# Layer attention of the last two latent blocks behind the first query, and 40 PEER steps more in the second tail

## What is computed

```python
def block(args):                      # window attention, one block of 128 queries
    qi, ki, vi, mi = args
    s_loc = where(mi, einsum(qi, ki) * scale, -inf)      # its own block and both neighbours
    s_ctx = einsum(qi, k_ctx) * scale                    # and all 256 context tokens
    p = softmax_with_sink(concatenate([s_loc, s_ctx]), sink_l)
    return einsum(p[..., :n_loc], vi) + einsum(p[..., n_loc:], v_ctx)

def merge(ys, gates_pre, w_branch, w_out):               # four branches, attention is ys[3]
    acc = sum(sigmoid(gates[i]) * (ys[i] @ w_branch[i]) for i in range(4))
    return acc @ w_out

def block(xb):                        # PEER, one block of 128 tokens
    s = einsum(xb @ wq, keys32)                          # 8 heads, 2 x 128 keys
    expert, cv = top 16 of the 16 x 16 sums of the two top-16 lists
    act = gelu(einsum('nd,nhkd->nhk', xb, u[expert]))    # 128 rows of u for every token
    return einsum('nhk,nhkd->nd', softmax(cv) * act, v[expert])
```

## Time and profile before

| | |
|---|---|
| runs, median (lowest to highest) | 6053.19 us (6052.09 to 6063.03) |
| profiled execution, span | 6280.9 us |
| TensorE, VectorE, ScalarE, GpSimd busy | 4128.8, 3226.1, 711.8, 2794.8 us |
| DMA | 1739.24 MB, 277 GB/s over the span |
| gathers of u and v | 2560, of 512 KB each |

### The profile page before, as it was taken

How to read it: one execution, slowest core, us unless ns; L and a number is a source line. 1 busy time by engine, 2 the same in 40 slices (tenths; PEclk the granted TensorE clock), 3 DMA queues, 4 the chain that set the end, 5 groups by cost and what they waited for, 6 DMA issues and landing times.

```text
span 6280.9 us, 65214 instructions
## 1 busy us (share of the span) xinstructions
PE 4128.8 (66%) x23760; PEld 2525.3 (40%) x23760; DVE 3226.1 (51%) x7726; ACT 711.8 (11%) x1572; POOL 2794.8 (44%) x2606
## 2 busy tenths in 40 slices
PE   5899767777988864544443668888977533333346
PEld 4677544335666652221110235557766300000012
DVE  3422788565625856556444216443277564654430
ACT  1221112123010011000000001233100000000000
POOL 0000243555322446767767630000034677777765
PEclk8999887889998986665555789999988755555557
DMA  6645565988886999999999971112579999999998
GB/s 221 219 156 166 190 208 199 316 312 291 290 302 231 323 340 343 355 352 360 361 367 361 368 262 43 57 43 80 171 257 326 348 353 361 369 358 365 359 367 328
DMA packets 721231, 1739.24 MB, mean 277 GB/s; under 512 B 88912, under 2 KB 371408, under 8 KB 719248
## 3 DMA queue, kind: packets, MB, share of 16 engines
q0 software_dynamic: 380032, 1384.49, 59.9%
q1 hardware_dynamic: 314896, 304.03, 15.4%
q10 hardware_dynamic: 25984, 46.56, 2.1%
HBM read 1706.98 MB, written 27.89 MB: 276 GB/s over the span
## 4 chain that ended last, share of the span: by engine, by line
PE 31%; issue 21%; DMA 10%; POOL 10%; DVE 9%; another core or an unknown queue 2%; ACT 2%; SPq 0%; POOLq 0%; ACTq 0%; DVEq 0%
POOL arena L3090 10%; PE bank L1219 7%; PE bank L1312 6%; DMA arena<-in_peer_v,arena 5%; PE bank L794 4%; PE bank L1273 3%; PE bank L1225 3%; DMA arena<-in_peer_u,arena 3%; DVE arena L2252 2%; PE bank L805 1%; PE bank L876 1%; PE bank L1174 1%; DMA arena<-in_w_in 1%; PE bank L1253 1%
## 5 line engine op out<-in xcount | busy, mean ns | idle before, releaser
L3090 POOL DMA_INDIRECT arena<-in_peer_u,arena x1280 | 1413.4, 1104 | 2173.6 <-DVE arena L2162 951.5
L1312 PE MATMUL bank<-arena 128*32 128x256 f32 x10240 | 1216.4, 541 | 1451.7 <-DMA arena<-in_peer_v,arena 1175.5
L2252 DVE CUSTOM_DVE_ANT_0 arena<-arena 128x1024 f32<-128x1024 f32 x1280 | 1540.5, 1223 | 1013.7 <-DMA arena<-in_peer_u,arena 922.4
L3090 POOL DMA_INDIRECT arena<-in_peer_v,arena x1280 | 1354.6, 1058 | 880.6 <-PE bank L1312 357.6
L1312 PEld LDWEIGHTS bank<-arena 128*32 128x32 f32 x10240 | 311.2, 130 | 2306.7 <-DMA arena<-in_peer_v,arena 1705.3
L1219 PE MATMUL bank<-arena 128*128 128x256 f32 x2560 | 618.3, 397 | 90.7 <-issue 55.8
L794 PE MATMUL bank<-arena 128*128 128x512 f32 (+1 forms) x1600 | 636.9, 552 | 30.2 <-issue 26.6
L1219 PEld LDWEIGHTS bank<-arena 128*128 128x128 f32 x2560 | 504.8, 200 | 187.1 <-issue 108.7
L794 PEld LDWEIGHTS bank<-arena 128*128 128x128 f32 x1600 | 320.4, 207 | 299.5 <-issue 279.4
L1225 PE MATMUL bank<-arena 128*128 128x256 f32 x1280 | 306.5, 382 | 2.3 <-ACT arena L2810 2.3
L1273 PE MATMUL bank<-arena 128*128 128x256 f32 x1280 | 292.6, 390 | 23.2 <-issue 23.2
(11 more groups left out here) (271 smaller groups left out, 3905.3 us busy)
## 6 DMA issues: line engine op xcount, KB each, us to landing
arena<-in_w_in SPq DMA_DIRECT2D x152, 1024.0 KB
arena<-in_mod_w POOLq DMA_DIRECT2D x20, 2048.0 KB, 11.6
arena<-in_peer_wq SPq DMA_DIRECT2D x40, 1024.0 KB
arena<-in_w_branch SPq DMA_DIRECT2D x60, 512.0 KB
arena<-in_w_out SPq DMA_DIRECT2D x20, 1024.0 KB
arena<-in_peer_u,arena POOLq DMA_INDIRECT x1280
arena<-in_peer_v,arena POOLq DMA_INDIRECT x1280
arena<-in_w_branch SPq DMA_DIRECT2D x40, 256.0 KB
```

What stands on the lines that cost most here:

```text
L1312: i = mm(banks[6 + g // 2][32 * j:32 * j + 32, (g % 2) * W:(g % 2 + 1) * W], G["ws"][:, g, 32 * m:32 * m + 32], G["row"][ROW_BUFFER["v", i ...
L2252: v.tensor_tensor_reduce(u, u, G["h2"][it % 2], 1.0, 0.0, ALU.mult, ALU.add, G["dots"][:, n:n + 1]).then_inc(*pr.step("dot", it, n))
L3090: fl.done(eng.indirect_dma_start(G["row"][x], None, table, bass.IndirectOffsetOnAxis(ids[:, n:n + 1], 0)), f"row_landed{x}", (kind + "_lan ...
```

## The change

`attn_mix` takes a half. Before the first tail it now treats blocks 2 and 3 alone (10 units instead of 18). Blocks 4 and 5 are treated at the start of the second tail, 10 units, woven with three of the four branches of that half's merge; the fourth branch follows. There attention takes PSUM banks 0, 1, 2, 6 and 7 and the woven merge banks 3 and 4.

The second tails take ROUTE + 128 + 40 steps of their PEER call, c1 and the part behind t1 40 fewer. For the first 44 slots of the call's second block four u and four v buffers are used. GpSimd's wait for the end of the second query is moved from that block's slot 0 to its slot 44. The routing of the third block is moved from slots 3 to 80 of the second block to slots 43 to 96.

In layer 0 the place of attention's keys and values is used by others in between, so ScalarE's queue stores both (384 KB each) to HBM ahead of the first half and loads them back at the start of the second tail, behind peer0's last store of x. In both layers attention's scores lie over WSP and its keys, values and diagonal over YP and XS; WSP is cleared at slot 116 of a call's first block instead of ahead of the call. The weights of the second half's merge are loaded with the fourth branch last.

```diff
@@ constants and tables @@
+BESIDE = {"attn": (0, 1, 2, 6, 7), "merge": (3, 4)}
...
+AHEAD = 40
+SWITCH = AHEAD + 4
+
+
+def ahead_of(call, it):
+
+    return 0 if call is PC0 or it != call.first + 1 else AHEAD
+
+
+def route_table(start):
+
+    if start == 0:
+        heads = {(16 * (j // 2) + 8 * (j % 2) + k): (what, j) for j in range(HEADS) for k, what in ((3, "keys"), (7, "pairs"))}
+        return {**heads, 64: ("centre",), 68: ("pick", 0), 76: ("pick", 1), 80: ("experts",), 119: ("gates",)}
+    heads = {start + 3 + 5 * j + k: (what, j) for j in range(HEADS) for k, what in ((0, "keys"), (3, "pairs"))}
+    return {**heads, start + 44: ("centre",), start + 46: ("pick", 0), start + 52: ("pick", 1), start + 56: ("experts",),
+            119: ("gates",)}
...
-                for kind, ring, i, step in (("u", u_ring, it, "dot"), ("v", v_ring, it - 1, "v_summed")):
+                few = ahead_of(call, it) and n < SWITCH
+                for kind, ring, i, step in (("u", u_ring[:4] if few else u_ring, it, "dot"),
+                                            ("v", v_ring[:4] if few else v_ring, it - 1, "v_summed")):
...
-                attn_mix=4 * nb + 2, merge=48)
+                attn_mix=4 * len(halves_of(p)[0]) + 2, merge=48)
...
-    if woven(p) and f == 0:
-        return [x for x in every if x[1] < 3], [x for x in every if x[1] == 3]
     if late(p) and f == 0:
         return [x for x in every if x[1]], [x for x in every if x[1] == 0]
-    return [every]
+    return [x for x in every if x[1] < 3], [x for x in every if x[1] == 3]
...
+        ATTN_LOW = SLOTS * 32 + NSCORE + W
...
-            k, v_, s_, pt, dg = lay_low(0, *sizes) if woven(p) else lay(base, *sizes)
+            if woven(p) or f:
+                (s_, pt), (k, v_, dg) = lay_low(0, *sizes[2:4]), lay_low(ATTN_LOW, *sizes[0:2], sizes[4])
+            else:
+                k, v_, s_, pt, dg = lay(base, *sizes)
@@ TensorE @@
-            def attn_mix(p):
+            def attn_mix(p, half):
...
-                seq = [(t, f) for t in blocks_of(p) for f in range(AH // AKV)]
+                seq = [(blocks_of(p)[x], f) for x in halves_of(p)[half] for f in range(AH // AKV)]
+                kept, ring = late(p) and half, "attn" if half else None
+                if kept:
+                    eng.wait_ge(*at("y_scaled", PC0.first + len(PC0.blocks) - 1))
...
-                if p.t0:
+                if kept:
+                    eng.wait_ge(*at("attn_back", p.l))
+                elif p.t0:
                     eng.wait_ge(*at("attn_in", p.l))
...
-                pn, half = p.name, slice(f * W, (f + 1) * W)
+                pn, half, ring = p.name, slice(f * W, (f + 1) * W), "merge" if f and part[0][1] == 0 else None
...
+                        if it == call.first:
+                            for x in (6, 7):
+                                eng.wait_ge(*at("read", last_in[x]))
@@ TensorE, VectorE and ScalarE alike @@
-                yield from weave(attn_mix(p), merge_part(p, 0, merge_parts(p, 0)[0]), u["merge"] / u["attn_mix"])
+                yield from weave(attn_mix(p, 0), merge_part(p, 0, merge_parts(p, 0)[0]), u["merge"] / u["attn_mix"])
                 yield from tail(p, 0)
 
             def tail(p, f):
+                if f:
+                    u = units(p)
+                    yield from weave(attn_mix(p, f), merge_part(p, f, merge_parts(p, f)[0]), u["merge"] / u["attn_mix"])
                 yield from merge(p, f)
...
-            side_by_side("t0", tail(L0, 1), side, ROUTE + SLOTS, 1.0)
-            side_by_side("c1", mixer(C1), side, 3 * SLOTS, 1.0)
+            side_by_side("t0", tail(L0, 1), side, ROUTE + SLOTS + AHEAD, 1.0)
+            side_by_side("c1", mixer(C1), side, 3 * SLOTS - AHEAD, 1.0)
...
-            side_by_side("t1", tail(L1, 1), side, ROUTE + SLOTS, 1.0)
-            for _ in first(side, 2 * SLOTS + FINAL_AFTER):
+            side_by_side("t1", tail(L1, 1), side, ROUTE + SLOTS + AHEAD, 1.0)
+            for _ in first(side, 2 * SLOTS + FINAL_AFTER - AHEAD):
@@ VectorE @@
-                v.memset(WSP, 0.0).then_inc(*pr.step("spread_zero", call.name))
...
+                                if n == SLOTS - 12 and it == first:
+                                    if call is not PC0:
+                                        eng.wait_ge(*at("full", ("ay", scored_in, call.blocks[-1], AH // AKV - 1)))
+                                    v.memset(WSP, 0.0).then_inc(*pr.step("spread_zero", call.name))
...
-                                    route_part(it + 1, h, k)
+                                    route_part(it + 1, n, ahead_of(call, it))
@@ ScalarE @@
+                if late(p) and half == 0:
+                    eng.wait_ge(*at("ak_roped", pn, 0))
+                    eng.wait_ge(*at("attn_in", p.l))
+                    eng.wait_ge(*mn.latest())
+                    dma(keptd[:, 0:TOK], A["K"], "attn_all_kept")
+                    dma(keptd[:, TOK:2 * TOK].rearrange("p (t d) -> p t d", t=NB), A["V"], "attn_all_kept", ("attn_all_kept", p.l))
+                if late(p) and half:
+                    eng.wait_ge(*at("attn_all_kept", p.l))
+                    eng.wait_ge(*at("x_stored", PC0.first + len(PC0.blocks) - 1))
+                    dma(A["K"], keptd[:, 0:TOK], "attn_back")
+                    dma(A["V"], keptd[:, TOK:2 * TOK].rearrange("p (t d) -> p t d", t=NB), "attn_back", ("attn_back", p.l))
...
-                            if n == 0 and it + 1 <= last:
+                            if n == ahead_of(call, it) and it + 1 <= last:
                                 scores_in(it + 1)
@@ GpSimd @@
-                    if it == call.first + 1 and call is not PC0:
-                        for e in ENG:
-                            eng.wait_ge(*at("end", e, ("query1", "l0" if call is PL0 else "l1")))
-                        eng.sem_inc(fl.sem("gathers_allowed"), 1)
                     for n in range(SLOTS):
+                        if ahead_of(call, it) and n == SWITCH:
+                            for e in ENG:
+                                eng.wait_ge(*at("end", e, ("query1", "l0" if call is PL0 else "l1")))
+                            eng.sem_inc(fl.sem("gathers_allowed"), 1)
```

More of the change, by code:

```diff
@@ L214, in late, with tail_stages @@
     return p.name == "l0"
+def tail_stages(p):
+    return [f"{x}{f}" for f in range(len(halves_of(p))) for x in ("attn",) * f + ("merge", "out", "query")]
 def pass_stages(p):
@@ L219, in pass_stages @@
         s = ["norm", "conv", "ret0", "rets0", "rets1", "mlss0", "mlss1", "attn"]
-        return s + [f"{x}{f}" for f in range(len(halves_of(p))) for x in ("merge", "out", "query")]
+        return s + tail_stages(p)
     s = ["norm"]
@@ L224, in pass_stages @@
     s += ["rows", "mlss0", "mls1", "mlss1", "attn"] + ["conv"] * late(p)
-    return s + ([f"{x}{f}" for f in range(len(halves_of(p))) for x in ("merge", "out", "query")] if p.out else [])
+    return s + (tail_stages(p) if p.out else [])
 STAGES = [("mod", "mod")] + [(s, p.name) for p in PASSES for s in pass_stages(p)] + [("final", "final")]
@@ L750, in build @@
         banks_of = {} if known is None else known["banks"]
-        last_in, taken = {}, {"next": 0, "banks": BANKS}
+        last_in, taken = {}, {"next": 0, "banks": BANKS, "attn": 0, "merge": 0}
         def bank_of(name):
@@ L1401, in _ @@
             side, costs = peer(PL1), []
-            side_by_side("t1", tail(L1, 1), side, ROUTE + SLOTS, 1.0, costs)
+            side_by_side("t1", tail(L1, 1), side, ROUTE + SLOTS + AHEAD, 1.0, costs)
             fl.marks[("cost", "t1")] = costs
@@ L2195, in weigh, with route_part @@
                         .then_inc(*pr.step("weighed", it, h))
-                def route_part(it, h, k):
-                    if h == 0 and k == 3:
+                def route_part(it, n, start):
+                    what, *j = route_table(start).get(n, ("nothing",))
+                    if what == "keys" and j[0] == 0:
                         eng.wait_ge(*at("scores_in", it))
-                    if h < HEADS // 2 and k in (3, 11):
-                        top_keys(pr, G, SCO, 2 * h + k // 8)
-                    if h < HEADS // 2 and k in (7, 15):
-                        candidates(pr, G, 2 * h + k // 8)
-                    if h == HEADS // 2 and k == 0:
+                    if what == "keys":
+                        top_keys(pr, G, SCO, j[0])
+                    if what == "pairs":
+                        candidates(pr, G, j[0])
+                    if what == "centre":
                         centre(pr, G, it)
-                    if h == HEADS // 2 and k in (4, 12):
-                        pick_keys(pr, G, k // 8)
-                    if h == HEADS // 2 + 1 and k == 0:
+                    if what == "pick":
+                        pick_keys(pr, G, j[0])
+                    if what == "experts":
                         experts(pr, G, l, it)
-                    if h == HEADS - 1 and k == 7:
+                    if what == "gates":
```

86 lines of the change are left out of this document (48 added, 38 removed).

## The result

| | before | after |
|---|---|---|
| runs, median (lowest to highest) | 6056.02 us (6052.09 to 6063.03, 4 runs) | 6125.08 us (6118.80 to 6126.18, 4 runs) |
| ratio | | 1.0122, 95% interval 1.0103 to 1.0141 |
| profiled execution, span | 6280.9 us | 6122.7 us |

The two spans can't be subtracted: the runs came from more than one chip, the kernel before takes 6050 to 6056 us on some and 6257 us on another, and the profile shown ahead of the prediction is of the slower kind. I had expected its second tails at 325 to 335 us; they take 319.

What follows compares the result with a forecast made beforehand. Gathers bound the kernel behind the tails, TensorE layer 1's attention, three close limits the second tails. Terms -46 - 52 + 4 + 14 + 2 + 40 = -38 us, scaled to -37, gave 6016 us, range 5940 to 6095.

Steps and rivals of the forecast that it cites:

- Layer 1's attention: Stretch without gathers in layer 1: eight of 18 attention units leave, 46 us saved, bounds 34 to 60.
- the handover: Start of the next PEER call: routing waits behind attention's first unit, +4 us in layer 1, +14 in layer 0.
- Layer 0's attention: Layer 0 ahead of its merge: 71 us leave, 19 moved PEER steps cost 19, so 52 us saved, bounds 15 to 60.
- fourth rival: Layer 0 gives nothing, moved steps and denser dealing costing as much as attention leaves: 6066 us, chance 0.13.
- Part A: Second tail, slots up to 80 of the call's first block: 216 us, VectorE 186 busy, DMA share 0.80.
- Part B: Rest of a second tail behind slot 80: 258 us of DMA work at share 0.96, so 269 us.
- The dip of 7 us at the switch: DMA share of 0.82 over 50 us in a second tail, expected to go with eight gathers in flight: -7 us.
- the second, 0.20: Second tails: gathers starve through two merge banks and VectorE's load, 530 us a tail, 6103 us in all, chance 0.20.
- The signs that I had named for a wrong forecast: Tail above 504 us, waits for VectorE's L2020, clock under 0.8 there, or gathers idle for layer 0's keys beyond 25 us.
- The first rival: Second tails stay full at DMA share 0.97, as VectorE overlaps better: 5937 us, chance 0.12.
- the fifth: The change doesn't act, another chain than TensorE's setting the end of query 0: 6053 us, chance 0.03.
- The third: TensorE's clock falls to 0.62 late in the second tails, 299 us there instead of 269: 6074 us, chance 0.05.

Runs made afterwards that it cites:

- e2: The kernel after with attention left where it was, all ahead of the first tail, the 40 steps still dealt into the second tails: 6048.68 us, 0.9992.
- e0: The kernel before, unchanged, profiled again beside the first experiments: 6056.14 us, span 6054.3 us.
- e3: The kernel after, but in the second tails attention comes first by itself, then the merge with all five banks: 6100.78 us, 1.0085 of the kernel before.

## Why the prediction was wrong

Layer 1's attention, **right**: -46 forecast, with +4 for the handover -42; measured -48, of which the stretch from the last score of the first query to the first gather is +1. (Attention there lies at 4195 to 4416 in the profile ahead of the prediction and not at 4200 to 4425, 221 us for 225.) The merge without attention kept its 380 ns a matmul.

Layer 0's attention, **wrong by the price of a moved step, and by the stretch that was scaled**. For a step I took 1.0 us between 0.60 and 2.95, "nearest the first", because the merge had TensorE at 1.00. Measured are 2.4 us, near the upper bound of two gathers: 39 us for 16 steps where I had 19 us for 19. The steps did not go "above all to the full merge": four did, at 3.1 us each, and ten went ahead of attention, at 2.5. The 71 us were 8/18 of a window of 160 us, 1385 to 1545; attention lies at 1376 to 1524 there, 148 us, and the 42 steps of the window are 37 in attention. On the chips of the result the same stretch takes 122 us, and 53 go. (On a chip like that of the first profile 71 us do go, so there only the steps' price is off.) Forecast with the handover -38, measured -8 in one pair of executions and -2 in the mean over nine. The handover itself was right: +14 forecast, +13 measured in the means. This was the outcome of the fourth rival, which I gave 0.13.

The length of a second tail, **right, in part by luck**: 485 us forecast, 490 measured, from parts that are 8 us too long and 13 us too short. Part A 208 us for 216, with VectorE busy 184 for 186 and a DMA share of 0.85 for 0.80. The DMA work of 431 us came out at 0.85 x 208 + 0.85 x 144 + 0.95 x 138 = 430, in part by luck too: by the same measure the work before was 307 us and not 317, and the tail holds 85 more gathers and not 80. Part B was 282 us for 269: I put 0.96 over all of it, and its first half has 0.85, the waits for weights (W) that I had not named.

What the tail was compared with, **wrong, and the step that turned the sign**. My windows, 4595 to 4935 and 1996 to 2337, begin 12 to 15 us ahead of the first gather and end 6 to 11 us behind the last matmul of scores; the 485 us were built up from the first gather on. By the same measure a tail before is 318 us in the very profile I read (2008.4 to 2325.9, 4610.4 to 4928.9), and not 340. That put 22 us of gain into each tail, and it also watered down the DMA share: the earlier trace rows show 0.90 to 0.96, while cut at the first gather the tails stood at 0.95 and 0.98, and at 0.96 and 0.91. Here they are in the profile ahead of the prediction, columns as in the earlier trace rows:

```profile
2008.00:2226.00 218.00, 173.06 (x712) 146.05 (x713) 172.36 (x450) 13.15 (x35) 105.12 (x87) 0.88 0.95 333
2226.00:2326.00 100.00, 86.26 (x427) 76.24 (x426) 67.76 (x129) 17.05 (x31) 48.91 (x41) 0.93 0.98 351
4610.00:4828.00 218.00, 171.61 (x720) 145.12 (x719) 173.06 (x450) 13.43 (x35) 103.32 (x87) 0.90 0.96 333
4828.00:4929.00 101.00, 87.31 (x426) 76.92 (x424) 67.43 (x129) 17.10 (x31) 50.00 (x41) 0.92 0.91 325
```

There was next to no idle transfer time for 80 more gathers to use, and in e2 they lengthened a tail by as much as they gave back behind it.

What the 80 gathers give back, **too high**: 118 us from 1.476 us each; behind the tails the time fell by 107 and 113, since these chips gather in 1.35 us (742 in 1000 us in e0). Scaling the sum by 6053/6281 hid that this is one term's error and not all terms'. The dip of 7 us at the switch brought nothing that can be seen: 80 x 1.35 = 108 is all of peer1's difference.

The errors add up, in us against the pair of executions of the table: layer 0 +30, layer 1 -6, the tails 42 (base), 11 (length), 17 (worth of a gather), 14 (dip) and 2 less for the routing, which is in the tails: together 106 us, the distance from -38 to +68.

Of the rivals, the second, 0.20, had the outcome (6103 forecast, 6125 measured) and half of the mechanism: GpSimd does starve on VectorE's dots, but from VectorE's load and from weights that come late. The two banks are, by e3, at most a small part of it. Its break-even of 504 us lies, with the base alone put right, near 482, and 490 is past it. The signs that I had named for a wrong forecast did not come: the tail stayed under 504 us, the waits for L2020 (L2066 in the kernel after) are 3 us in the first part, the clock stayed above 0.8, and the handover grew by less than 25 us. They watched the tail after, and the error was in the tail before. The first rival falls by the DMA share of 0.85, the fifth by layer 1's stretch, which is 48 us shorter. The third falls: the granted clock was 0.88, 0.82 and 0.87 in the three parts, with TensorE busy 0.74, 0.65 and 0.75 of them, so the rule of the Trainium skill (TensorE: Matmul & The Clock Gate, What's actually happening) that idleness brings the throttle back agrees in sign with this trace and did not come near 0.62.

## What to carry to other kernels

Cut a stretch of before at the same events at which the stretch of after will be cut: windows with round edges took 15 us of idle ahead of the first gather for room inside the tail. When work is taken from beside a stream that is dealt by cost, count the steps that move with it and price them at the pace of the stream: 16 steps took back 39 of 53 us here. A stretch with the DMA share at 0.95 took in 80 more gathers only one for one. And two moves that are each near neutral (+0.2% and -0.1%) cost 1.2% together, where both draw on the engine whose queue frees the buffers, so run them apart first: here the half in layer 1 alone was a gain of 0.4%.

## What was not expected of the hardware

The same kernel takes 6050 or 6257 us, 3.4% apart, depending on the chip (two of the chips of the experiments are of the one kind, one of the other). Most of it lies where the gathers run with little beside them: 1.35 to 1.36 us a gather (393 GB/s) on the one kind and 1.46 to 1.48 (362 GB/s) on the other, for the second. There are 99 us of it in the rest of peer1 and 103 behind layer 1's tail, between e0 and the profile ahead of the prediction. Another 26 us lie in layer 0's attention, 122 us in e0 and 148 there:

```profile
1376.00:1524.00 148.00, 108.53 (x1104) 84.73 (x1103) 97.41 (x217) 65.46 (x159) 73.56 (x75) 0.88 0.78 259
```

So the room that I had read in that stretch (DMA share 0.82) is smaller on the chips of the result, where the share is 0.89. Other stretches are the same on both: layer 1 without gathers 891.8 and 893.5 us, and a second tail 318.5 and 318.6, though its DMA share is 0.95. A share near 1 therefore does not say that a stretch hangs on the gather rate; what makes this tail the same on both is not shown. Against a change that trades gather time for engine time the chip matters, and a profile has to be compared with one of its own kind.
